# The MLP input product of a decoder trunk as products of 64 rows on the two halves of the TensorE array

## The reference, cut to what matters

```
h = rms_norm(x, g_pre_mlp)
y = jnp.square(jax.nn.relu(h @ w_mlp_in)) @ w_mlp_out
return x + rms_norm(y, g_post_mlp)
```

## Time and profile before

| | |
|---|---|
| time, median of 3 runs | 816.87 us (816.37 to 818.72) |
| the profiled execution | 818.21 us |
| its span, first to last instruction | 816.5 us |
| TensorE busy in the span | 804.5 us (99%), 4622 matmuls |
| VectorE busy | 482.4 us (59%) |
| ScalarE busy | 403.9 us (49%) |
| GpSimd busy | 56.8 us (7%) |
| HBM read | 144.31 MB, 178 GB/s over the span |

### The profile page before, as it was taken

How to read it: one execution, slowest core, us unless ns; L and a number is a source line. 1 busy time by engine, 2 the same in 40 slices (tenths; PEclk the granted TensorE clock), 3 DMA queues, 4 the chain that set the end, 5 groups by cost and what they waited for, 6 DMA issues and landing times.

```text
span 816.5 us, 12007 instructions
## 1 busy us (share of the span) xinstructions
PE 804.5 (99%) x4622; PEld 699.2 (86%) x4622; DVE 482.4 (59%) x627; ACT 403.9 (49%) x619; POOL 56.8 (7%) x88
## 2 busy tenths in 40 slices
PE   8999999999999999999999999999999999999997
PEld 6897788887889999999879887888878899999995
DVE  4588445449786555555575775444697755555553
ACT  4565555543465544445455655554436654444441
POOL 2010000005110000000020100000152000000000
PEclk9999999999999999999999999999999999999999
DMA  7796445465366655655655963456544575565531
GB/s 225 211 286 201 140 155 154 157 204 157 108 183 229 199 173 189 203 180 188 201 147 181 280 194 110 153 154 198 185 132 154 179 231 177 186 205 180 181 128 51
DMA packets 85404, 145.89 MB, mean 179 GB/s; under 512 B 4949, under 2 KB 50405, under 8 KB 85366
## 3 DMA queue, kind: packets, MB, share of 16 engines
q1 hardware_dynamic: 85334, 145.33, 56.6%
q0 software_dynamic: 32, 0.05, 0.0%
HBM read 144.31 MB, written 1.05 MB: 178 GB/s over the span
## 4 chain that ended last, share of the span: by engine, by line
PE 93%; DVE 3%; POOL 1%; ACT 1%; issue 1%; POOLq 0%; DVEq 0%; ACTq 0%
PE banks L1150 28%; PE banks L1152 28%; PE banks L1151 28%; DVE w_lo L716 1%; PE banks L1162 1%; PE banks L1220 1%; PE banks L1193 1%; PE banks L1228 1%; PE banks L1219 1%; DVE rows L732 1%; PE banks L1170 1%; POOL ms L1105 1%; POOL rstd L1110 0%; PE banks L1288 0%; PE banks L1340 0%
## 5 line engine op out<-in xcount | busy, mean ns | idle before, releaser
L716 DVE TENSOR_TENSOR w_lo<-raw,w_hi 128x1024 fp32r<-128x1024 f32 (+1 forms) x272 | 315.5, 1197 | 156.5 <-ACT w_hi L444 155.8
L444 ACT CAST w_hi<-raw 128x1024 fp32r<-128x1024 f32 (+1 forms) x272 | 263.7, 1013 | 143.2 <-PE banks L1152 116.4
L1150 PE MATMUL banks<-w_hi,xT_hi 128*128 128x512 f32 (+2 forms) x480 | 181.9, 379 | 0.8 <-DVE xT_lo L739 0.8
L1152 PE MATMUL banks<-w_hi,xT_lo 128*128 128x512 f32 (+2 forms) x480 | 178.3, 371 | 0.0
L1151 PE MATMUL banks<-w_lo,xT_hi 128*128 128x512 f32 (+2 forms) x480 | 178.0, 371 | 0.0
L1150 PE MATMUL banks<-xT_hi,w_hi 128*128 128x256 f32 x576 | 164.0, 285 | 0.1
L1152 PE MATMUL banks<-xT_hi,w_lo 128*128 128x256 f32 x576 | 163.0, 283 | 0.0
L1151 PE MATMUL banks<-xT_lo,w_hi 128*128 128x256 f32 x576 | 163.0, 283 | 0.0
L1150 PE MATMUL banks<-w_hi,brT_hi 128*128 128x512 f32 x320 | 125.1, 391 | 0.0
L1151 PE MATMUL banks<-w_lo,brT_hi 128*128 128x512 f32 x320 | 124.8, 390 | 0.0
L1152 PE MATMUL banks<-w_hi,brT_lo 128*128 128x512 f32 x320 | 124.5, 389 | 0.0
(11 more groups left out here) (173 smaller groups left out, 524.2 us busy)
## 6 DMA issues: line engine op xcount, KB each, us to landing
raw<-in_w_in_dram SPq DMA_DIRECT2D x96, 512.0 KB, 4.5
raw<-in_w_mlp_in_dram SPq DMA_DIRECT2D x64, 512.0 KB, 4.3
raw<-in_w_mlp_out_dram SPq DMA_DIRECT2D x64, 512.0 KB, 4.3
raw<-in_w_branch_dram SPq DMA_DIRECT2D x16, 512.0 KB, 4.2
raw<-in_w_out_dram SPq DMA_DIRECT2D x16, 512.0 KB, 3.8
raw<-in_w_in_dram SPq DMA_DIRECT2D x16, 176.0 KB, 3.3
x<-in_x_dram SPq DMA_DIRECT2D x4, 256.0 KB, 4.7
gain_pre<-in_g_pre_mlp_dram SPq DMA_DIRECT2D x2, 512.0 KB, 5.8
```

The costliest lines, as they stand in the source:

```text
L444: nc.scalar.copy(w_hi[:, c % RING, h * n:(h + 1) * n], raw[:, q % RAW, 0:n]).then_inc(hi_ready, 1)
L716: v.tensor_tensor(w_lo[:, c % RING, cut], raw[:, q % RAW, 0:n], w_hi[:, c % RING, cut].bitcast(F32), ALU.subtract).then_inc(lo_ready, 1)
L1150: nc.tensor.matmul(dst, l_hi, r_hi, start=first, stop=False)
L1152: return nc.tensor.matmul(dst, l_lo, r_hi, start=False, stop=last)
```

## The change

Every product of `mlp_in` (steps 2 to 15) is made of two: rows 0 to 63 of the weight block with rows 0 to 63 of `xT`, and rows 64 to 127 with rows 64 to 127. Each has 128 stationary columns and 256 moving columns as before. The two halves accumulate in banks of their own: banks 4 and 5 for even k, 6 and 7 for odd k. ScalarE copies the second bank to SBUF (`hidden_part`), VectorE adds the first bank to it, then takes relu and square in one instruction (`max` with 0, then `mult`); ScalarE rounds that to `brT_hi`, and VectorE makes `brT_lo`. In the loops the round and the low part stand between the two halves of the split of chunk c+3. The steps 0 and 1 keep ScalarE's relu and square. The output product, the weights, the DMAs and all other stages stay.

```diff
+            def feature_major_rows(l, c, bank, f):
+                hi, lo = both(c)
+                cut = slice(f * P, (f + 1) * P)
+                for kt in range(KT):
+                    pairs = ((hi, xT_hi), (hi, xT_lo), (lo, xT_hi))
+                    for n, (w, xs) in enumerate(pairs):
+                        for r in range(2):
+                            part = slice(64 * r, 64 * r + 64)
+                            last = nc.tensor.matmul(psum[:, bank + r, f * S:(f + 1) * S], w[part, kt, cut], xs[part, kt, :],
+                                                    start=(kt, n) == (0, 0), stop=(kt, n) == (KT - 1, 2))
+                return last
...
                 def mlp_in(k, c, i=0, f=None):
                     wait_chunk(l, c, i)
-                    return feature_major(l, c, 4 + k % 2, f)
+                    for n in range(2) if f is None else (f,):
+                        last = feature_major_rows(l, c, 4 + 2 * (k % 2), n)
+                    return last
...
+                def hidden_copy_part(k, i=0):
+                    act.wait_ge(chunk_used, used(l, C_MLP + 2 * k - (2 if k == STEPS - 1 else 1) + 4 * i))
+                    act.wait_ge(relu_ready, nth(l, STEPS, k - 1 + 2 * i))
+                    bank = 4 + 2 * (k % 2)
+                    nc.scalar.copy(hidden_part, psum[:, bank + 1, :]
+                                   ).then_inc(part_copied, 1)
+
+                def hidden_round(k, i=0):
+                    act.wait_ge(hidden_squared, nth(l, STEPS, k + 2 * i))
+                    nc.scalar.copy(brT_hi[:, hidden_slot(k):hidden_slot(k) + 2, :].rearrange("p f n -> p (f n)"),
+                                   hidden_sq).then_inc(hidden_hi_ready, 1)
...
                         split(l, c + 2, i)
-                        hidden_hi(2 + b, i)
-                        split(l, c + 3, i)
+                        hidden_copy_part(2 + b, i)
+                        split_half(l, c + 3, 0, i)
+                        hidden_round(2 + b, i)
+                        split_half(l, c + 3, 1, i)
...
-                def hidden(k, i=0):
+                def hidden_square(k, i=0):
                     if k >= 1:
                         dve.wait_ge(hidden_lo_ready, nth(l, STEPS, k - 1 + 2 * i))
+                    if k >= 2:
+                        dve.wait_ge(part_copied, nth(l, STEPS - 2, k - 2 + 2 * i))
+                        bank = 4 + 2 * (k % 2)
+                        v.tensor_tensor(hidden_relu[:, k % 2, :], psum[:, bank, :], hidden_part, ALU.add
+                                        ).then_inc(relu_ready, 1)
                     dve.wait_ge(relu_ready, nth(l, STEPS, k + 2 * i))
-                    v.tensor_tensor(hidden_sq, hidden_relu[:, k % 2, :], hidden_relu[:, k % 2, :], ALU.mult
-                                    ).then_inc(hidden_squared, 1)
+                    v.scalar_tensor_tensor(hidden_sq, hidden_relu[:, k % 2, :], 0.0, hidden_relu[:, k % 2, :],
+                                           ALU.max, ALU.mult).then_inc(hidden_squared, 1)
```

More of the change, by code:

```diff
@@ L106, in hybrid_trunk @@
         hidden_sq = rows[:, 0:512]
+        hidden_part = rows[:, 1536:2048]
         hidden_relu = rows[:, 512:1536].rearrange("p (b n) -> p b n", b=2)
@@ L259, in hybrid_trunk @@
         hiddenT_psum = sem("hiddenT_psum")
+        part_copied = sem("part_copied")
         relu_ready = sem("relu_ready")
@@ L664, in _, with hidden_hi @@
                 hidden_copy(1)
[L666 to L675, removed]
-                                         ).then_inc(relu_ready, 1)
-                    act.wait_ge(relu_ready, nth(l, STEPS, k + 2 * i))
-                    nc.scalar.activation(brT_hi[:, hidden_slot(k):hidden_slot(k) + 2, :].rearrange("p f n -> p (f n)"),
-                                         hidden_relu[:, k % 2, :], ACT.Square).then_inc(hidden_hi_ready, 1)
+                def hidden_hi(k):
+                    act.wait_ge(hiddenT_psum, nth(l, 2, k))
+                    nc.scalar.activation(hidden_relu[:, k, :], psum[:, 1 + 2 * k, :], ACT.Relu
+                                         ).then_inc(relu_ready, 1)
+                    act.wait_ge(relu_ready, nth(l, STEPS, k))
+                    nc.scalar.activation(brT_hi[:, 2 * k:2 * k + 2, :].rearrange("p f n -> p (f n)"),
+                                         hidden_relu[:, k, :], ACT.Square).then_inc(hidden_hi_ready, 1)
+                def hidden_copy_part(k, i=0):
[8 more added lines that the diff above has]
+                                   hidden_sq).then_inc(hidden_hi_ready, 1)
                 hidden_hi(0)
@@ L687, in _ @@
                         split(l, c + 2, i)
-                        hidden_hi(2 + b, i)
-                        split(l, c + 3, i)
+                        hidden_copy_part(2 + b, i)
+                        split_half(l, c + 3, 0, i)
+                        hidden_round(2 + b, i)
+                        split_half(l, c + 3, 1, i)
                 split(l, CHUNKS - 2)
-                hidden_hi(STEPS - 2)
+                hidden_copy_part(STEPS - 2)
+                hidden_round(STEPS - 2)
                 split(l, CHUNKS - 1)
-                hidden_hi(STEPS - 1)
+                hidden_copy_part(STEPS - 1)
+                hidden_round(STEPS - 1)
                 if l + 1 < L:
@@ L1033, in _, with hidden_low @@
                 split(l, C_LOOP)
[L1035 removed]
+                def hidden_square(k, i=0):
                     if k >= 1:
                         dve.wait_ge(hidden_lo_ready, nth(l, STEPS, k - 1 + 2 * i))
+                    if k >= 2:
[3 more added lines that the diff above has]
+                                        ).then_inc(relu_ready, 1)
                     dve.wait_ge(relu_ready, nth(l, STEPS, k + 2 * i))
[L1041 to L1042 removed]
+                    v.scalar_tensor_tensor(hidden_sq, hidden_relu[:, k % 2, :], 0.0, hidden_relu[:, k % 2, :],
+                                           ALU.max, ALU.mult).then_inc(hidden_squared, 1)
+                def hidden_low(k, i=0):
                     dve.wait_ge(hidden_squared, nth(l, STEPS, k + 2 * i))
@@ L1049, in hidden @@
                                     ).then_inc(hidden_lo_ready, 1)
-                hidden(0)
-                hidden(1)
+                for k in range(2):
+                    hidden_square(k)
+                    hidden_low(k)
                 split(l, C_LOOP + 1)
@@ L1057, in _ @@
                         split(l, c + 2, i)
-                        hidden(2 + b, i)
-                        split(l, c + 3, i)
+                        hidden_square(2 + b, i)
+                        split_half(l, c + 3, 0, i)
+                        hidden_low(2 + b, i)
+                        split_half(l, c + 3, 1, i)
                 split(l, CHUNKS - 2)
-                hidden(STEPS - 2)
+                hidden_square(STEPS - 2)
+                hidden_low(STEPS - 2)
                 split(l, CHUNKS - 1)
-                hidden(STEPS - 1)
+                hidden_square(STEPS - 1)
+                hidden_low(STEPS - 1)
                 if l + 1 < L:
```

## The result

The changed kernel takes 828.99 us (median of 4 runs, 827.75 to 830.07), the kernel before in the same comparison 817.68 us (4 runs, 816.37 to 818.72). The ratio is 1.0143, with a 95% interval of 1.0127 to 1.0160: 11.3 us slower, where 10.2 us was forecast.

The account below looks back on a forecast made before the run. TensorE, busy 99% of the span, was taken as the bound: products 0 plus ways in and out 10.2 us, on the median 816.87, gave 827.1, stated as 827 us. The forecast's own range was 820 to 832.

Parts of the forecast that it names:

- The products: MLP input products on TensorE: both row halves overlap fully, each pair keeping 0.120 us; cost 0.
- the spatial gate's row: Earlier trace, column halves: 16 instructions in 1.15 us, read as two tiles at once, distances 0.059 us each.
- the first rival: MLP input products: the 0.013 us remainder of each matmul disappears but for 0.002; -14.8 us, 812.3 in all; chance 0.24.
- the second: Rival for MLP input products: the halves' remainders add, 0.1335 us a pair; +18.1 us, 845.2 in all; chance 0.12.
- the third: Rival for MLP input products: halves take turns, 0.224 or 0.240 us a pair; 966.9 or 988.4 us in all; chance 0.19.
- The way in and out: Switching TensorE between 128 and 64 rows around each input product: 0.34 us each, 30 times, +10.2 us.
- The head of 64 rows: Earlier trace, projection to first value matmul: 1.56 us against 1.21 for 96 rows, so 0.34 to 0.35 per stay.
- this rival: MLP input products: a half's next load cannot overlap its own matmul, 0.107 + 0.107 us each; near 960 us, no separate chance.
- The signs: Expected in the MLP trace: pairs 0.01 to 0.03 us apart, input product +0.34 us, uncovered first loads, +5 us per layer, no waits.
- ScalarE and VectorE: MLP hidden values: VectorE gets 21 us more, `brT_lo` ready after 4.1 to 4.3 us, all hidden; no cost.

Follow-up runs that it names:

- e2: Like e1, but the first matmul of each step's input product is two halves, 28 pairs in all; 828.08 us, ratio 1.0125 to the kernel before.
- e3: Changed kernel with halves only for features f = 0 of each step and whole products for f = 1, 672 pairs; 827.65 us, ratio 1.0119.
- e5: Changed kernel without the products of rows 64 to 127, 1344 matmuls of 64 rows; 828.02 us, ratio 1.0135 to the kernel before.
- e6: Changed kernel with both matmuls of each pair on rows 0 to 63, into two banks; 989.55 us, ratio 1.2112 to the kernel before.
- e4: Changed kernel with blocks kt 0 to 3 as halves and 4 to 7 whole, 56 ways in and out; 838.76 us, ratio 1.0258.
- e1: Changed kernel with all MLP input products whole again, keeping the second bank and the added ScalarE and VectorE work; 818.09 us, ratio 1.0000.
- e8: Changed kernel with halves ordered by turns of 24 matmuls, all of one half's f before the other's; 958.69 us, ratio 1.1734.
- e9: Changed kernel with the same matmuls, the halves ordered by turns of twelve; 915.92 us, ratio 1.1212 to the kernel before.
- e7: Changed kernel with the same matmuls, the halves ordered by turns of three for each kt; 829.94 us, ratio 1.0159 to the kernel before.

## Why the prediction was right

**The products: 0 was forecast, and it is 0.** This was the likeliest case and not a sure one: no row of before had halves of rows at work together. Pairs stand 0.12 apart in the changed kernel, e2 and e3 differ by 644 pairs and not in time, and e5 without the second half is as slow as with it. The reading of the spatial gate's row as two tiles at work held for rows as it does for columns. The 0.013 us that each matmul takes beyond its columns stayed with each half, so the first rival did not come; nor did it add up, so the second did not. e6 shows that two matmuls take turns only when they use the same rows, so the third did not come either.

**The way in and out: 0.34 was forecast, 0.38 it is.** Of this comes the difference of 11.3 and 10.2 us: 30 x 0.38 = 11.4. The head of 64 rows, from which I took it, goes back to the whole array with a transposition, whose first distance is lengthened by less: three transposes last 0.55 us there against 0.49 in the other head, 0.06, where the output product loses 0.11. I had compared the two stages as if their borders were those of the MLP; why the transposes lose less is open. I had also read 103.64 and 103.76 in the earlier trace rows as two matmuls of one kind. They are the second L1219 and the first L1220. The two of L1219 start at 103.43 and 103.64, 0.21 us apart where the head of 96 rows has 0.11: that is the late first load, 0.10 us, which I had not named. That the cost does not depend on what is computed inside the stay, only on the number of stays, is shown by e2 to e4.
The Trainium skill, "TensorEngine Tiling (Array Packing)", Key Properties, has TensorE drain at a change of mode, and the 0.09 us at each border agree with it. The weight load that is not issued ahead, 0.11 us at each border, is the larger part of the cost.
The sentence of "TensorE: Matmul & The Clock Gate", Part 3, in the Trainium skill, that a load overlaps a matmul only where the row group differs, would have made e5's distance about 0.22, an estimate from a load of 0.11 and 0.107 of columns. It is 0.12: the load of a half runs under that half's own matmul. The prediction's time for this rival, near 960 us, comes to 953 by its own terms (816.87 + 10.2 + 0.094 x 1344).

**The signs.** PEld is idle before the first load of all 30 ways in, 0.13 to 0.35 us each. TensorE waits for nothing in the loops of either MLP (the profiled run has two waits for `w_lo` outside them, 0.7 us together, which e1 and e3 do not have). The stretch from the first to the last matmul of in(2) to in(15) grows from 151.9 us to 157.3 in each layer, by 5.4 where 5 was forecast. Two signs were off: the halves of a pair start 0.003 to 0.004 us apart and not 0.01 to 0.03, and an input product is 0.19 us longer and not 0.34, because the other half of the cost falls into the output product behind it.

**ScalarE and VectorE: nothing was forecast, and nothing came.** e1 is the proof. The timeline of the hidden in the loop after the change, first ACT, for the earlier trace rows:

```profile
302.55 0.59 ACT L682 COPY rows<-banks 128x512 f32<-128x512 f32 x1 [3.73 <-PE banks L1177]
...
304.63 0.62 ACT L687 CAST brT_hi<-rows 128x512 fp32r<-128x512 f32 x1 [0.54 <-DVE rows L1059]
```

and DVE:

```profile
303.17 0.69 DVE L1056 TENSOR_TENSOR rows<-banks,rows 128x512 f32<-128x512 f32 x1 [2.91 <-ACT rows L682]
303.90 0.69 DVE L1059 SCALAR_TENSOR_TENSOR rows<-rows 128x512 f32<-128x512 f32 x1
304.51 1.22 DVE L729 TENSOR_TENSOR w_lo<-raw,w_hi 128x1024 fp32r<-128x1024 f32 x1
305.65 0.68 DVE L1067 TENSOR_TENSOR brT_lo<-rows,brT_hi 128x512 fp32r<-128x512 f32 x1
```

`brT_lo` is ready 3.78 us after the copy began (302.55 to 306.33), against 4.1 to 4.3 in the text. Relu with square is 0.69 and not 0.75. The 28 adds take 0.69 us each, 19.4 us, and the page has only 15 us more for VectorE (497.5 against 482.4), where 21 was forecast: neighbouring instructions overlap in the trace (303.90 + 0.69 is past 304.51, and 304.51 + 1.22 past 305.65), and the page counts such time once. At the end of the second layer, for the earlier trace rows:

```profile
809.09 0.69 DVE L1067 TENSOR_TENSOR brT_lo<-rows,brT_hi 128x512 fp32r<-128x512 f32 x1 [0.76 <-ACT brT_hi L687]
```

It ends at 809.78. The first matmul of out(15) is this one:

```profile
811.68 0.39 PE L1175 MATMUL banks<-w_hi,brT_hi 128*128 128x512 f32 x1
```

1.9 us are left, where 1.7 was forecast.

**What stays open.** Why each float32r matmul takes 0.013 us beyond its columns; e5 shows only that a half alone has it too. Why the first load is not issued ahead across a border. Halves of columns were not run with float32r.

## What to carry to other kernels

Two products on different rows of the array run at once, but each half still has to pass its columns: when a product already fills all 128 rows, splitting it gives nothing. A gain is to be looked for where the rows are short to begin with: two matmuls of 64 rows took 0.24 us on the same rows (e6) and 0.12 on different ones. No kernel with such products was changed here. What costs is each change between 64 and 128 rows, 0.38 us for a way in and out in this kernel, whatever is done inside; so count such borders first, and put products of one kind together. An extra add and copy beside a full TensorE were free here: their chain took 3.8 us, and its reader came about 17 us after its start.

## What the runs showed of the hardware that I had not expected

TensorE starts matmuls out of the program's order when the other half of the rows is free, past three waiting matmuls: in e8 the other half starts beside the 21st of 24, in e9 beside the 9th of 12, and turns of three (e7) overlap wholly. It did not look further than that in e8 and e9. Whether the limit counts matmuls alone or their weight loads too was not tested. In e8 and e9 a group that starts in this way gets its first weights 0.11 us late.
